# Experts sorted by token count: four passes of 128 slots with three products, four of 64 slots with two, in blocks of 1024 columns

## Chip, core and metric

The kernel runs on one core of one Trainium2 chip. The metric is the device time of one execution in microseconds (us), lower is better. Engines are named as in the profile: TensorE (PE, with its weight loads as PEld), VectorE (DVE), ScalarE (ACT), GpSimd (POOL), and SyncE (SP), which issues the weight loads from memory.

## What is computed

Two post-norm layers over 256 tokens of 1024 values, all in float32. Each has a mixer (pooling and mLSTM) and a channel mixer. The channel mixer of layer 0 is a dense SwiGLU, that of layer 1 takes two of eight experts for each token:

```python
N_EXPERTS = 8
TOP_K = 2
D_FF_EXPERT = 7 * D_MODEL // 2      # 3584

def swiglu(x, wg, wu, wd):
    return (jax.nn.silu(x @ wg) * (x @ wu)) @ wd

def moe_swiglu(x, w_router, b_router, wg, wu, wd):
    logits = (x @ w_router).astype(jnp.float32) + b_router.astype(jnp.float32)
    top_v, top_i = lax.top_k(logits, TOP_K)
    top_w = jax.nn.softmax(top_v, axis=-1)
    combine = jnp.sum(jax.nn.one_hot(top_i, N_EXPERTS, dtype=jnp.float32) * top_w[..., None], axis=-2)
    out = jnp.zeros_like(x)
    for e in range(N_EXPERTS):
        out = out + combine[..., e:e + 1] * swiglu(x, wg[e], wu[e], wd[e])
    return out
```

512 pairs of token and expert are spread over the eight experts as the router chooses. The biases of the router are drawn, so that experts get unequal numbers.

## The kernel before

Weights come from memory in units of 128 x 2048 values (1 MB). For each unit SP issues one transfer (`load`, L443), ScalarE rounds it into `w_hi` (`round_hi`, L644), VectorE subtracts that from the raw values into `w_lo` (`subtract_lo`, L865), and TensorE multiplies: a product in float32 is made of three matmuls in the rounded type, hi x hi, hi x lo, lo x hi (`product`, L1288 to L1292). Raw units lie in a ring of RING = 9 slots (7 of their own, RAW, and 2 in space that the expert stage does not use), and the pairs w_hi, w_lo in a ring of SPLIT = 3. ScalarE waits for the matmuls of the unit three before, VectorE for ScalarE, TensorE for VectorE, SP for VectorE's subtraction of the unit that had the slot (`slot_free`, L428). At the change from one item to the next, the first unit of the new item has the slot of unit 36 of the old one, of 42. Every engine has its own program in order.

An expert is one item, in the order 0 to 7. Its tokens are gathered into CAP = 104 slots; where an expert had more, further items are appended (MAX_OVER), for which GpSimd builds a table (`overflow_items`, L593, semaphore `table_ready` at L620). An item runs over seven blocks of 512 hidden columns. A block has two gate units, two up units (banks 2, 3 or 6, 7 in turn) and two down units, which stand one block later and add into banks 0 and 1. The tokens are the stationary operand (104 columns), the weights the moving one (512 columns), 12 matmuls a unit, 42 units an item. Between units stand, at steps written out by hand (STEP_ constants):

- silu of the gate bank by ScalarE (L824), product with the up bank by VectorE (L1232), four transposes by TensorE (L1617), the hi part of these by ScalarE (L829) and the lo part by VectorE (L1237);
- the scatter of the item before: sums `y_sb` (ScalarE, L841, two copies) times the slot matrix (L1576) and an addition into `work` for each quarter (L1218);
- picks for the next item by VectorE (`build_pick`, L1197: it waits for `table_ready`, then copies its table row at L1200 and compares at L1160 and L1162), and its gather (L1564): 16 float32 matmuls of tokens with the 0/1 pick matrix, recorded as 32, then hi and lo (L814, L1209).

Item 0 is written out; 1 to 7 are a loop. Before item 0 stand router, top two, positions (L1127 to L1172), the first picks and the first gather. In item 0, VectorE makes the tables (`item_tables`, L1175) after unit 4 and the scaled residual (`start_sums`, L1192, L1195) after unit 9. After item 7 come the last scatter, the last norm and the output.

## Time and profile before

| | |
|---|---|
| Time, median of 3 runs | 1494.95 us (1488.65 to 1495.79) |
| Span of the profiled execution | 1495.0 us |
| Busy: PE, PEld | 1434.3 us (96%), 1131.2 us (76%) |
| Busy: DVE, ACT, POOL | 1157.2 us (77%), 912.4 us (61%), 175.8 us (12%) |
| Granted TensorE clock, mean | 0.972 of full |
| Moved by DMA | 424.68 MB, mean 284 GB/s |

The span is cut by time: mixer 0, dense mixer and mixer 1 up to about 440 us, then the expert stage to 1476, then the tail. Busy PE says only that matmuls overlap in the records; what a matmul costs is the distance from one start to the next. An engine's idle time is given with what ended it.

### The profile page before, as it was taken

How to read it: one execution, taken by the hardware profiler on the slowest of the kernel's cores; microseconds unless marked ns; L12 is line 12 of the kernel's file. 1: busy time of each engine (PE TensorE's matmuls, PEld its weight loads, DVE VectorE, ACT ScalarE, POOL GpSimd, SP SyncE). 2: the span in 40 equal slices, each digit the busy share in tenths (PEclk: the TensorE clock that was granted, in tenths of full speed). 3: DMA queues.
4: the chain of work that ended last, by engine and by line, in shares of the span. 5: the costliest groups of instructions: out<-in, count | busy, mean ns of one | idle time of the engine just before them, and what ended most of it. 6: DMA issues, size and time to landing. Idle time of an engine off the chain costs nothing.

```text
span 1495.0 us, 19658 instructions
## 1 busy us (share of the span) xinstructions
PE 1434.3 (96%) x7356; PEld 1131.2 (76%) x7356; DVE 1157.2 (77%) x991; ACT 912.4 (61%) x736; POOL 175.8 (12%) x224
## 2 busy tenths in 40 slices
PE   8998999988989869999999999999999999999996
PEld 7888999977977647777777777777777777777773
DVE  6766545468578668887988888888798978878887
ACT  5434434446436646676767767677676776767664
POOL 4523000025524810000000000000000000000001
PEclk9998999989989979999999999999999999999998
DMA  9635555544348867997999899799799979979970
GB/s 333 233 117 172 194 176 194 185 153 144 111 156 311 321 226 247 394 394 259 381 394 346 293 393 394 243 394 395 277 360 396 387 250 395 393 254 385 393 289 30
DMA packets 182307, 424.68 MB, mean 284 GB/s; under 512 B 9280, under 2 KB 11616, under 8 KB 182256
## 3 DMA queue, kind: packets, MB, share of 16 engines
q1 hardware_dynamic: 180608, 419.17, 77.3%
q0 software_dynamic: 1504, 4.76, 1.0%
q8 instruction: 33, 0.54, 0.1%
q14 instruction: 18, 0.15, 0.0%
q10 hardware_dynamic: 144, 0.07, 0.0%
HBM read 422.92 MB, written 1.05 MB: 284 GB/s over the span
## 4 chain that ended last, share of the span: by engine, by line
PE 86%; DVE 6%; POOL 4%; issue 2%; ACT 1%; DMA 1%; SPq 0%; POOLq 0%; DVEq 0%; ACTq 0%
PE bank L1290 26%; PE bank L1292 26%; PE bank L1291 26%; PE bank L1564 2%; DVE w_lo L868 2%; POOL arena L599 2%; PE bank L1576 2%; PE bank L1617 1%; DVE arena L940 1%; DMA raw<-in_w_in 1%; PE bank L1427 1%; POOL arena L607 1%; PE bank L1311 0%; DVE x_lo L895 0%; DVE arena L938 0%
## 5 line engine op out<-in xcount | busy, mean ns | idle before, releaser
L868 DVE TENSOR_TENSOR w_lo<-raw,w_hi 128x2048 fp32r<-128x2048 f32 x335 | 767.8, 2295 | 234.9 <-ACT w_hi L649 231.5
L649 ACT CAST w_hi<-raw 128x2048 fp32r<-128x2048 f32 x335 | 639.7, 1910 | 249.4 <-PE bank L1292 246.1
L1290 PE MATMUL bank<-w_hi,parts 128*104 128x512 f32 (+1 forms) x1496 | 603.6, 403 | 17.2 <-DVE w_lo L868 17.1
L1292 PE MATMUL bank<-w_hi,parts 128*104 128x512 f32 (+1 forms) x1496 | 588.0, 393 | 0.0
L1291 PE MATMUL bank<-w_lo,parts 128*104 128x512 f32 (+1 forms) x1496 | 587.6, 393 | 0.0
L1290 PEld LDWEIGHTS bank<-w_hi,parts 128*104 128x104 f32 (+1 forms) x1496 | 254.5, 170 | 109.8 <-DVE w_lo L868 17.7
L1291 PEld LDWEIGHTS bank<-w_lo,parts 128*104 128x104 f32 (+1 forms) x1496 | 254.8, 170 | 92.6 <-issue 7.3
L1292 PEld LDWEIGHTS bank<-w_hi,parts 128*104 128x104 f32 (+1 forms) x1496 | 254.4, 170 | 90.6
L1290 PE MATMUL bank<-x_hi,w_hi 128*128 128x256 f32 x596 | 173.0, 290 | 1.4 <-ACT arena L707 1.4
L1291 PE MATMUL bank<-x_lo,w_hi 128*128 128x256 f32 x596 | 171.7, 288 | 0.0
L1292 PE MATMUL bank<-x_hi,w_lo 128*128 128x256 f32 x596 | 171.6, 288 | 0.0
L868 DVE TENSOR_TENSOR w_lo<-arena,w_hi 128x2048 fp32r<-128x2048 f32 x64 | 146.5, 2290 | 27.8 <-ACT w_hi L649 27.2
L586 POOL TENSOR_TENSOR tokens<-work,ln_row 128x1024 f32<-128x1024 f32 x7 | 16.6, 2370 | 1195.0 <-DVE work L1076 1195.0
L649 ACT CAST w_hi<-arena 128x2048 fp32r<-128x2048 f32 x64 | 122.3, 1911 | 43.9 <-PE bank L1292 43.9
L1290 PEld LDWEIGHTS bank<-x_hi,w_hi 128*128 128x128 f32 x596 | 117.9, 198 | 3.3 <-issue 3.0
L1291 PEld LDWEIGHTS bank<-x_lo,w_hi 128*128 128x128 f32 x596 | 117.7, 198 | 0.2
L1292 PEld LDWEIGHTS bank<-x_hi,w_lo 128*128 128x128 f32 x596 | 117.5, 197 | 0.0
L824 ACT ACTIVATE arena<-bank 104x512 f32<-104x512 f32 x56 | 33.5, 598 | 79.6 <-PE bank L1292 79.5
L829 ACT CAST parts<-bank 128x416 fp32r<-128x416 f32 x56 | 28.3, 506 | 54.1 <-PE bank L1617 54.1
L1564 PE MATMUL bank<-arena,tokens 128*128 128x104 f32 x288 | 37.2, 287 | 1.1 <-DVE arena L1160 1.1
L1232 DVE TENSOR_TENSOR arena<-arena,bank 104x512 f32<-104x512 f32 x56 | 38.1, 680 | 0.0
L1564 PEld LDWEIGHTS bank<-arena,tokens 128*128 128x128 f32 x288 | 36.5, 203 | 2.0 <-issue 1.1
(196 smaller groups left out, 809.0 us busy)
## 6 DMA issues: line engine op xcount, KB each, us to landing
raw<-in_wu_exp SPq DMA_DIRECT2D x96, 1024.0 KB, 7.4
raw<-in_wd_exp SPq DMA_DIRECT2D x96, 1024.0 KB, 7.1
raw<-in_wg_exp SPq DMA_DIRECT2D x80, 1024.0 KB, 7.0
arena<-in_wg_exp SPq DMA_DIRECT2D x32, 1024.0 KB, 7.6
raw<-in_w_in SPq DMA_DIRECT2D x20, 1024.0 KB, 6.7
arena<-in_wu_exp SPq DMA_DIRECT2D x16, 1024.0 KB, 9.4
arena<-in_wd_exp SPq DMA_DIRECT2D x16, 1024.0 KB, 9.1
raw<-in_wg_dense SPq DMA_DIRECT2D x11, 1024.0 KB, 5.1
```

What stands on the lines that cost most here:

```text
L586: st.then(g.tensor_tensor(tokens[:, t, :], work[:, t, :], ln_row[:, 0, :], ALU.mult))
L599: st.then(g.tensor_tensor(v[..., 0:n], v[..., 0:n], v[..., n:2 * n], ALU.add))
L649: a.copy(w_hi[:, n % SPLIT, :], slot(n)).then_inc(hi_ready, 1)
L824: a.activation(esg[0:CAP, b % 2, :], bank[(2, 6)[b % 2]][0:CAP, :], ACT.Silu) \
L829: a.copy(eh_hi[:, b % 2].rearrange("p j c -> p (j c)"), bank[5][:, 0:4 * CAP]) \
L868: v.tensor_tensor(w_lo[:, n % SPLIT, :], slot(n), w_hi[:, n % SPLIT, :].bitcast(F32), ALU.subtract).then_inc(lo_ready, 1)
L1232: v.tensor_tensor(eh[0:CAP, b % 2, :], esg[0:CAP, b % 2, :], bank[(3, 7)[b % 2]][0:CAP, :], ALU.mult).then_inc(eh_ready, 1)
L1290: mm(psum, left[0], right[0], start=first, stop=False)
L1291: mm(psum, left[0], right[1], start=False, stop=False)
L1292: return mm(psum, left[1], right[0], start=False, stop=last)
L1564: last = mm(psum[:, (k % 4) * CAP:(k % 4 + 1) * CAP], tokens[:, t, k * P:(k + 1) * P], pick[:, t, :], start=t == 0, stop=t == TT - 1)
L1576: mm(psum[:, :], scat[0:CAP, t * P:(t + 1) * P], y_sb[0:CAP, n * HALF:(n + 1) * HALF], start=True, stop=True).then_inc(scat_mm, 1)
```

## The change

- Experts are sorted by their token counts on the chip. The four largest take the even items (0, 2, 4, 6) with 128 slots and three matmuls a product as before; the four smallest take the odd ones with 64 slots. An expert that has more than its item holds gets a further item of 128 slots at the end (`n_over`).
- In a narrow item the hi part of 64 tokens and their lo part stand side by side as 128 stationary columns, so a product is two matmuls, with w_hi and w_lo (`one_pass`). The lower 64 rows of each gate and up bank are then copied by ScalarE to `fold` and added to the upper rows by a matmul with a shifted identity.
- The seven blocks of 512 columns become three of 1024 and one of 512. Gate is in banks 2 and 3, up in 6 and 7; copies, silu and products have up to 1024 columns. Of the sums there is one copy, of 1024 columns.
- Transposes of a wide block are made in two steps, into banks 5 and 4; their hi and lo parts are copied from there.
- Tokens are split once into `xt_hi` and `xt_lo` (ScalarE, VectorE), and the gather multiplies these, in the rounded type. Of the gathered tokens ScalarE copies both parts; VectorE has no step there, but for item 0.
- The table is made on VectorE in small steps after units 3 to 19 of item 0, and GpSimd has no part in it. SP waits for it before item 1 and takes each item's expert number from it.
- `start_sums` stands before item 0; after it the tokens' buffer serves as ninth raw slot. RAW is 6, RING stays 9.
- The loop holds two items, a narrow and a wide one.

The core of the diff (in `narrow_item`, the first is ScalarE's, the second VectorE's, the third TensorE's):

```diff
-EXP_BLOCKS = F_EXP // FBLK
+EBLK = 1024
+EXP_WIDTH = [EBLK, EBLK, EBLK, 512]
+EXP_BLOCKS = len(EXP_WIDTH)
...
-CAP = 104
-MAX_OVER = (TOP_K * T) // (CAP + 1)
...
+WIDE, NARROW = 128, 64
+ITEM_CAP = [WIDE, NARROW, WIDE, NARROW, WIDE, NARROW, WIDE, NARROW]
+ITEM_RANK = [0, 4, 1, 5, 2, 6, 3, 7]
+MAX_OVER = 4
...
+PAIRS = E // 2 - 1
...
-RAW = 7
-RING = RAW + 2
+RAW = 6
+RING = RAW + 3
...
+TURN = {10: 0, 20: 1, 32: 2, 38: 3}
+SCATTER = {2: 0, 4: 1, 6: 2, 8: 3}
+STEP_SLOTS, STEP_PICK = 16, 20
+GATHER = {33: 0, 38: 1}
+TAKE = {36: 0, 40: 1}
...
-        spare = [arena[:, ARENA - UNIT:], arena[:, 0:UNIT]]
+        spare = [arena[:, ARENA - UNIT:], arena[:, 0:UNIT], tokens[:].rearrange("p t d -> p (t d)")]
...
-                return w[:, 4 * b + 2 * half:4 * b + 2 * half + 2, :]
-            return w[:, 4 * half:4 * half + 4, b * FBLK:(b + 1) * FBLK]
+                k0 = EBLK // P * b + 2 * half
+                return w[:, k0:k0 + 2, :]
+            kn = UNIT // EXP_WIDTH[b]
+            return w[:, kn * half:kn * (half + 1), b * EBLK:b * EBLK + EXP_WIDTH[b]]
...
+                elif u == RAW + 2:
+                    sp.wait_ge(tokens_free, 1)
...
             item_loads(0, 0, first=True)
+            sp.wait_ge(table_ready, 1)
             with sp.Fori(1, E) as i:
-                item_loads(i, i)
-
-            sp.wait_ge(table_ready, 1)
-            n_over = sp.value_load(over_int[0:1, MAX_OVER:MAX_OVER + 1], min_val=0, max_val=MAX_OVER)
+                e = sp.value_load(order_int[0:1, bass.ds(i, 1)], min_val=0, max_val=E - 1)
+                item_loads(i, e)
...
-            overflow_items()
...
+            def token_high(t):
+                act.wait_ge(tokens_ready, TT * 2 + t + 1)
+                a.copy(xt_hi[:, t, :], tokens[:, t, :]).then_inc(xthi_ready, 1)
...
+            def take(i, n, wide):
+
+                hi, lo = GATHER_BANKS[n]
+                act.wait_ge(gather_mm, 2 * i + n + 3)
+                if wide:
+                    a.copy(four(xg_lo, n), bank[lo])
+                a.copy(four(xg_hi, n), bank[hi]).then_inc(xg_ready, 1)
+
+            def gate_silu(i, b, rows):
+
+                if b:
+                    act.wait_ge(eh_ready, i * EXP_BLOCKS + b)
+                w = EXP_WIDTH[b]
+                a.activation(esg[0:rows, 0:w], wide_bank(GATE, w, rows), ACT.Silu).then_inc(esilu, 1)
+
+            def slots(i):
+                act.wait_ge(st_mm, i + 1)
+                a.copy(scat[:], bank[4][:, 0:T]).then_inc(scat_ready, 1)
+
+            def item_sums(i):
+                act.wait_ge(unit_done, i * ITEM_UNITS + (MOE_UNIT0 + ITEM_UNITS))
+                a.copy(y_sb[:], wide_bank(0, D)).then_inc(ysb_ready, 1)
...
+            def narrow_item(i, p, wide_next):
+                for u in range(ITEM_UNITS):
+                    round_hi(MOE_UNIT0 + u + AHEAD, i)
+                    if u in GATE_END or u in UP_END:
+                        act.wait_ge(unit_done, i * ITEM_UNITS + (MOE_UNIT0 + u + 1))
+                        b, n = (GATE_END[u], GATE) if u in GATE_END else (UP_END[u], UP)
+                        w = EXP_WIDTH[b]
+                        c0 = HALF if n == UP and w == HALF else 0
+                        if n == UP and w > HALF:
+                            act.wait_ge(fold_mm, 2 * EXP_BLOCKS * p + 2 * b + 1)
+                        elif n == GATE and b:
+                            act.wait_ge(fold_mm, 2 * EXP_BLOCKS * p + 2 * b)
+                        a.copy(fold[NARROW:, c0:c0 + w], psum[NARROW:, n:n + 2, :].rearrange("p a b -> p (a b)")[:, 0:w]) \
+                            .then_inc(foldin_ready, 1)
+                    if u - 1 in GATE_END:
+                        b = GATE_END[u - 1]
+                        act.wait_ge(fold_mm, 2 * EXP_BLOCKS * p + (2 * b + 1))
+                        if b == 0:
+                            act.wait_ge(eh_ready, i * EXP_BLOCKS)
+                        gate_silu(i, b, NARROW)
+                    if u in TURN:
+                        b = TURN[u]
+                        n, j = EXP_WIDTH[b] // P, 8 if b == EXP_BLOCKS - 1 else 0
+                        act.wait_ge(eturn_mm, i * FILLS + turned_fills(b))
+                        a.copy(eh_hi[:, j:j + n, 0:NARROW],
+                               bank[5][:, 0:n * NARROW].rearrange("p (j c) -> p j c", c=NARROW)) \
+                            .then_inc(ehi_ready, 2 if b < EXP_BLOCKS - 1 else 1)
+                    if u == STEP_SLOTS:
+                        slots(i)
+                    if u in TAKE:
+                        act.wait_ge(unit_done, i * ITEM_UNITS + (MOE_UNIT0 + u))
+                        take(i + 1, TAKE[u], wide_next)
+                item_sums(i)
...
+            def token_low(t):
+                dve.wait_ge(xthi_ready, t + 1)
+                v.tensor_tensor(xt_lo[:, t, :], tokens[:, t, :], xt_hi[:, t, :].bitcast(F32),
+                                ALU.subtract).then_inc(xtlo_ready, 1)
+
+            token_low(0)
...
+                if u == 3:
+                    wide_slots(lambda t: posm[:, t, 0:1], lambda t: comb[:, t, 0:1])
+                    dve.wait_ge(count_mm, 1)
+                    v.tensor_copy(count, bank[0][:, 4 * E:5 * E]).then_inc(count_ready, 1)
+                elif u == 4:
+                    dve.wait_ge(count_ready, 1)
+                    st.then(v.tensor_tensor(key, count, cst[:, C_BIG:C_BIG + E], ALU.add))
...
+                elif u == 19:
+                    st.add(v.tensor_copy(order_int[:, 0:MAX_ITEMS], item_tab[:, 0:MAX_ITEMS, 4]))
+                    st.then(v.tensor_copy(order_int[:, MAX_ITEMS:], n_over_f))
+                    dve.sem_inc(table_ready, 1)
 
             def start_sums():
-
-                dve.wait_ge(tokens_ready, TT * 3)
...
+                dve.sem_inc(tokens_free, 1)
...
+            def hidden(i, b, rows):
+
+                dve.wait_ge(esilu, i * EXP_BLOCKS + (b + 1))
+                w = EXP_WIDTH[b]
+                v.tensor_tensor(eh[0:rows, 0:w], esg[0:rows, 0:w], wide_bank(UP, w, rows), ALU.mult) \
+                    .then_inc(eh_ready, 1)
...
+            def narrow_item(i, p, wide_next):
+                for u in range(ITEM_UNITS):
+                    subtract_lo(MOE_UNIT0 + u + AHEAD, i)
+                    if u - 1 in UP_END:
+                        b = UP_END[u - 1]
+                        dve.wait_ge(fold_mm, 2 * EXP_BLOCKS * p + (2 * b + 2))
+                        dve.wait_ge(eturn_mm, i * FILLS + 2 * b)
+                        hidden(i, b, NARROW)
+                    if u in TURN:
+                        b = TURN[u]
+                        n, j = EXP_WIDTH[b] // P, 8 if b == EXP_BLOCKS - 1 else 0
+                        dve.wait_ge(ehi_ready, i * FILLS + turned_fills(b))
+                        v.tensor_tensor(eh_hi[:, j:j + n, NARROW:],
+                                        bank[5][:, 0:n * NARROW].rearrange("p (j c) -> p j c", c=NARROW),
+                                        eh_hi[:, j:j + n, 0:NARROW].bitcast(F32),
+                                        ALU.subtract).then_inc(elo_ready, 2 if b < EXP_BLOCKS - 1 else 1)
+                    if u - 1 in SCATTER:
+                        add_scattered(i - 1, SCATTER[u - 1])
...
+            start_sums()
...
+            def gather_half(parts_, n, psum, width, c0):
+                for k in range(4 * n, 4 * n + 4):
+                    at_c = (k % 4) * P + c0
+                    for t in range(TT):
+                        last = mm(psum[:, at_c:at_c + width], parts_[:, t, k * P:(k + 1) * P], pick[:, t, 0:width],
+                                  start=t == 0, stop=t == TT - 1)
+                return last
+
+            def gather(i, n, wide):
+
+                hi, lo = GATHER_BANKS[n]
                 if n == 0:
                     pe.wait_ge(pick_ready, 2 * i + 2)
-                for k in range(4 * n, 4 * n + 4):
-                    for t in range(TT):
-                        last = mm(psum[:, (k % 4) * CAP:(k % 4 + 1) * CAP],
-                                  tokens[:, t, k * P:(k + 1) * P], pick[:, t, :], start=t == 0, stop=t == TT - 1)
-                last.then_inc(gather_mm, 1)
+                if wide:
+                    gather_half(xt_hi, n, bank[hi], P, 0)
+                    gather_half(xt_lo, n, bank[lo], P, 0).then_inc(gather_mm, 1)
+                else:
+                    gather_half(xt_hi, n, bank[hi], NARROW, 0)
+                    gather_half(xt_lo, n, bank[hi], NARROW, NARROW).then_inc(gather_mm, 1)
...
+            def one_pass(psum, left, right, first, last):
+                mm(psum, left, right[0], start=first, stop=False)
+                return mm(psum, left, right[1], start=False, stop=last)
...
+            def narrow_item(i, p, wide_next):
+                for u in range(ITEM_UNITS):
+                    unit(i, u, False, one_pass, lambda k: xg_hi[:, k, :], lambda j: eh_hi[:, j, :])
+                    if u - 1 in GATE_END or u - 1 in UP_END:
+                        b, up = (GATE_END[u - 1], 0) if u - 1 in GATE_END else (UP_END[u - 1], 1)
+                        w = EXP_WIDTH[b]
+                        c0 = HALF if up and w == HALF else 0
+                        pe.wait_ge(foldin_ready, 2 * EXP_BLOCKS * p + (2 * b + up + 1))
+                        for hf in range(w // HALF):
+                            last = mm(bank[(GATE, UP)[up] + hf], shift, fold[:, c0 + hf * HALF:c0 + (hf + 1) * HALF],
+                                      start=False, stop=True, skip_group_check=True)
+                        last.then_inc(fold_mm, 1)
...
+            for n in range(2):
+                gather_half(xt_hi, n, bank[FIRST_BANKS[n][0]], P, 0).then_inc(gather_mm, 1)
+            pe.wait_ge(xtlo_ready, TT)
+            for n in range(2):
+                gather_half(xt_lo, n, bank[FIRST_BANKS[n][1]], P, 0).then_inc(gather_mm, 1)
+            wide_item(0, False, first=True)
+            with pe.Fori(0, PAIRS) as p:
+                narrow_item(p * 2 + 1, p, True)
+                wide_item(p * 2 + 2, False)
+            narrow_item(E - 1, PAIRS, True)
```

## Rows read from the trace of the kernel before

**Rows 1.** The line of the sum copies: count, duration in ns, first and last start.

```profile
L841 ACT COPY arena<-bank x16: 571/584/590, 593.7 to 1476.5; 104x512 f32<-104x512 f32 x16
```

**Rows 2.** Busy time by stretch: item 0 and items 1 to 7.

```profile
core 0: us, PE busy (x) PEld busy (x) DVE busy (x) ACT busy (x) POOL busy (x), PEclk, DMA share, GB/s
452.00:594.00 142.00, 124.92 (x570) 92.02 (x569) 104.68 (x77) 87.44 (x60) 54.07 (x99) 0.94 0.76 272
594.00:1476.00 882.00, 882.00 (x4020) 645.25 (x4019) 755.05 (x477) 618.29 (x421) 0.00 (x0) 1.00 0.93 343
```

**Rows 3.** Waits from 600 to 1470: who waited for whom, total, times, longest.

```profile
ACT w_hi L649 <- PE bank L1292: 151.9, 180, 2.3
DVE w_lo L868 <- ACT w_hi L649: 122.2, 152, 2.7
```

**Rows 4.** Timeline of TensorE (start us, us): 104 columns of weights, then 128.

```profile
861.12 0.39 PE L1291 MATMUL bank<-w_lo,parts 128*104 128x512 f32 x1
...
861.81 0.39 PE L1291 MATMUL bank<-w_lo,parts 128*104 128x512 f32 x1
...
409.39 0.39 PE L1290 MATMUL bank<-w_hi,parts 128*128 128x512 f32 x1
...
410.07 0.39 PE L1290 MATMUL bank<-w_hi,parts 128*128 128x512 f32 x1
```

**Rows 5.** Chain and timeline: four transposes, 16 gather records, eight scatter records.

```profile
551.13 0.36 PE bank L1617 x4
...
568.46 1.79 PE bank L1564 x16
...
1478.69 3.69 PE L1576 MATMUL bank<-arena 104*128 104x512 f32 x8 [2.21 <-issue]
```

**Rows 6.** Timeline of VectorE and TensorE, and the chain, at the hole of item 0.

```profile
531.46 0.17 DVE L1200 COPY arena<-arena 128x4 f32<-128x4 f32 x1 [17.98 <-POOLq L620]
...
534.87 0.76 PE L1290 MATMUL bank<-w_hi,parts 128*104 128x512 f32 x1 [17.07 <-DVE w_lo L868]
...
536.05 0.43 PE bank L1292
```

**Rows 7.** DMA: a stretch of 50 us, and GB/s in 40 slices of 860 to 960.

```profile
1000.00:1050.00 50.00, 50.00 (x222) 35.89 (x221) 43.44 (x31) 34.24 (x24) 0.00 (x0) 1.00 1.04 394
...
GB/s 387 387 388 398 408 400 388 386 388 386 412 404 391 388 385 389 402 405 400 386 388 386 397 403 406 387 389 387 388 406 352 400 328 280 0 0 12 291 170 365
```

**Rows 8.** Timeline: two casts, and two subtractions, one behind the other.

```profile
436.70 3.71 ACT L649 CAST w_hi<-raw 128x2048 fp32r<-128x2048 f32 x2
...
483.76 4.48 DVE L868 TENSOR_TENSOR w_lo<-raw,w_hi 128x2048 fp32r<-128x2048 f32 x2
```

**Rows 9.** Groups by line and shape: busy us, mean ns, idle before them.

```profile
L868 DVE TENSOR_TENSOR w_lo<-raw,w_hi 128x2048 fp32r<-128x2048 f32 x335 | 767.8, 2295 | 234.9 <-ACT w_hi L649 231.5
L649 ACT CAST w_hi<-raw 128x2048 fp32r<-128x2048 f32 x335 | 639.7, 1910 | 249.4 <-PE bank L1292 246.1 <-DMA raw<-in_w_in 2.7
...
L1291 PEld LDWEIGHTS bank<-w_lo,parts 128*104 128x104 f32 x1344 | 226.3, 168 | 87.0 <-issue 7.3
...
L1291 PEld LDWEIGHTS bank<-w_lo,parts 128*128 128x128 f32 x152 | 28.6, 188 | 5.6
...
L1232 DVE TENSOR_TENSOR arena<-arena,bank 104x512 f32<-104x512 f32 x56 | 38.1, 680 | 0.0
```

**Rows 10.** Timeline at the start of item 0, and of `start_sums`.

```profile
445.99 0.17 DVE L1170 RECIPROCAL arena<-arena 128x2 f32<-128x2 f32 x1
446.19 0.36 DVE L1172 TENSOR_SCALAR arena<-arena 128x8 f32<-128x8 f32 x2
...
451.82 0.46 PE L1290 MATMUL bank<-w_hi,parts 128*104 128x512 f32 x1
...
481.98 1.25 DVE L1195 TENSOR_SCALAR work<-tokens 128x2048 f32<-128x2048 f32 x1
```

**Rows 11.** Busy time in a stretch of mixer 1 with holes.

```profile
335.00:345.00 10.00, 8.59 (x72) 8.41 (x71) 5.71 (x10) 9.74 (x12) 2.78 (x1) 1.00 0.01 2
```

534 lines of the change are left out of this document (302 added, 232 removed).

## The prediction, made before the changed kernel was seen

> **What bounds the kernel now.** I read the stretches first [rows 1, 2]. The 16 copies of item sums run from 593.7 to 1476.5 us, two for each of eight items, so seven items take 882 us, 126.0 each [rows 1]. In that stretch TensorE is busy in all 882 us at the full granted clock, VectorE in 755, ScalarE in 618, and DMA moves 343 GB/s [rows 2]. The waits say the same from the other side: ScalarE waits for matmuls 151.9 us, VectorE for ScalarE 122.2, and TensorE appears in no large row [rows 3]. So an expert item is bound by matmul issue. Matmuls of 512 columns start 0.23 us apart (0.69 for three) [rows 4]. One item has 42 units of 12 of them, 504: 115.9 us. Beside them lie 28 transposes at 0.09 (2.5), the gather's 32 records at 0.112 (3.6) and the scatter's 8 at 0.46 with the last one's tail, 0.43 without (3.4) [rows 5]: 125.4 of 126.0. The first item is different: from 452 to 594 TensorE has 17.1 us without work [rows 2], and that is one hole: VectorE stands 17.98 us at L1200 for the table that GpSimd builds, TensorE follows with 17.07, and then runs at the low clock, matmuls 0.43 apart [rows 6].
>
> The other three resources of an item, since they come next. DMA: 42 units of 1.049 MB are 44.0 MB; the rate that is held for 50 us is 394 GB/s, and in the slices it goes between 385 to 389 and 400 to 412 [rows 7]. The fast slices recur as often as the down units, which come in rows of 4 KB where gate and up units have 2 KB. Two thirds at 387 and one third at 404 make 112.2 us an item. VectorE: a subtraction behind another takes 2.19 (4.48 less 2.29), 42 of them 92.0. ScalarE: a cast behind another 1.80, 42 make 75.6 [rows 8, 9].
>
> **The hole in item 0 goes.** GpSimd's table work is removed; VectorE does some 35 small operations of at most 128 elements, or 320 in one reduction, spread over units 3 to 19. Small operations take 0.17, dependent ones start 0.20 apart [rows 6, 10]; about 18 dependent ones at 0.21 and the rest at about 0.1 are 5.5 us where the old tables had about 1. What hides them is VectorE's idle time in a wide item, 882 less 755 over seven, 18 us each [rows 2]; without it they would cost 4.5. I take 0.5. Gone: 17.1 of hole and the low clock behind it, about 12 matmuls at 0.43 in place of 0.23, 2.4. GpSimd is free there, so nothing is late next; SP's new wait for the table stands behind unit 41's load, which itself waits for unit 32, long after unit 19. **-19.0.**
>
> **Start of the items.** Behind the first picks VectorE now also subtracts half of the tokens (1024 columns, 1.2 by the line from 0.68 at 512 to 2.29 at 2048 [rows 9]) and scales all tokens (1.25, before hidden at 482 [rows 10]), and both first copies of gathered tokens must be there before unit 0, where before the second one was waited for at unit 1. Chain: the combine weights are done at 446.6 [rows 10]; +1.2, +1.25, subtraction 2.2, copy 0.6, subtraction 2.2, copy 0.6 = 454.7, against 451.8 where unit 0 started [rows 10]. **+3.0** (0 to +5; the second unit is then ready at once, which can give some back). The ninth load slot is now the tokens' buffer, free at about 449; it is needed at unit 8, some 25 us later: nothing. Mixer and dense units get 6 raw slots for 7. A dense unit has 24 matmuls of 512 columns or 48 of half the length, 24 x 0.227 = 5.4 us, against 2.7 for its load (1.049 MB at 394): nothing, to +2.
>
> **Wide items, four.** 504 products as before, now with 128 columns of weights in place of 104. The weight loads grow from 168 to 188 ns, but with 128 columns matmuls start 0.227 apart (0.68 for three) against 0.23 [rows 4, 9]: the load lies beside the matmul before it. 504 matmuls: -1.5 to 0. Transposes 28 at 0.11 for 0.09: +0.6. The gather in two rounded halves is 32 matmuls of one pass for 16 of two: the same 32 records, of 64 or 128 columns; no row has such a one, the bounds are 0.05 and 0.12, so -2.0 to +0.3, and I take -0.5, near the weight-load bound of the 0.112. One copy of 1024 columns (about 1.07) ends the item where one of 512 (0.58) did: +0.5 if it shows. Gate and up banks are single now, but their readers run four units before the next writer, 11 us against 1.2. ScalarE's silu of 1024 columns stands 1.07 between two casts: cast n starts when matmuls n-3 end, cast and subtraction take 4.2, plus 1.07 is 5.3 against the 5.5 that two units of matmuls last, so it fits by 0.2 us; a slip of half a microsecond at 8 places is the upper end. **+0.5 each** (-2 to +4): 126.5.
>
> By the Trainium skill, TensorE: Matmul & The Clock Gate, section LDWEIGHTS, a weight load takes time by its columns, P/1.2 ns, so 24 more columns cost 20 ns. The trace agrees on the load itself (188 less 168) and shows that it is hidden; were it exposed, 504 loads would be 10.1 us an item and the total some 1470; with 0.227 measured, that is within rival 6's chance.
>
> **Narrow items, four.** Hi and lo tokens stand side by side in the 128 columns, so a unit has 8 matmuls for 12. TensorE: 336 at 0.23 = 77.3; 14 matmuls that fold the lower rows up, 3.2; transposes, gather, scatter 9. Sum 89.5, so 36 us under what it had. It no longer binds; the next three are:
> - DMA: gate and up units of 1024 columns have rows of 4 KB, 38 of 42 units at 404 and 4 at 387: 109.5; at the old mix 112.2. The lead of a full ring (four to six landed units when a wide item ends) lends some 10 us.
> - VectorE: 92.0 + products 3 x 1.22 + 0.68 + lo parts 2.4 + scatter sums 4 x 0.68 + picks 1.2, less 0.08 for each that follows another: 102.
> - ScalarE: 75.6 + 8 fold copies (6 x 1.07 + 2 x 0.6; a copy of 512 columns takes 0.58 [rows 1], each column more is put at the cast's slope, 1910 for 2048 [rows 9]) + silu 3.8 + hidden, gathered and slot copies 5 + sums 1.07, less overlap: 91.
>
> None of these is reached, since the three work in a ring of three split slots: cast n waits for matmuls n-3. From the end of subtraction n-3: matmuls 1.84, cast 1.91, two semaphore steps about 0.1 each, 3.95 until subtraction n can start; VectorE wants it at 2 x 2.19 = 4.4. Slack 0.45. A gate block puts a fold copy (1.07) and a silu (1.07) between ScalarE's casts, VectorE has nothing of its own there: it loses 2.1 - 0.45 and gains a little back, 1.2. An up block puts one fold copy in, followed by VectorE's own product: 0.4. A turn of the hidden values makes ScalarE wait for matmuls of this unit and the transposes: 0.4. Four blocks: 8; the end of the item with take and sum copies 1.5 to 2. 102 + 10 = 112, beside DMA at 109.5 to 112.2: I take **113**, 13.0 less than 126.0. Bounds: 107 (half of the stalls, lead used up) and 122 (twice the stalls).
>
> **Tail.** The last sum copy is 1024 wide: +0.5.
>
> **Sum.** 1495.0 - 19.0 + 3.0 + 4 x 0.5 - 4 x 13.0 + 0.5 = 1429.5, forecast 1430. The profiled span of 1495.0 is the median of the runs shown (1494.95), so nothing is added.
>
> **Rivals.**
> 1. The coupling costs twice (narrow 120 to 124): silu waits for the fold, the fold for ScalarE's copy, that for the unit's matmuls, and the chain of waits goes round the ring. For: slack 0.45 against insertions of 1.07. Against: VectorE's own extras let ScalarE catch up. 4 x 8 more: 1462. Chance 0.22.
> 2. DMA binds. Only if what DMA showed here, a mean of 343 [rows 2], were near what it can give: 44.0 MB at 350 are 126, narrow gains nothing over that, 1480. Against it: 394 over 50 us [rows 7]. Chance 0.07.
> The Trainium skill, DMA: Bandwidth & Descriptors, section Where 436 GB/s comes from, has this rule: from HBM to SBUF the HBM side binds at about 358 GB/s a core. An item would last 123 and the total would be 1470. The trace disagrees, with 394.
> 3. The floors are reached, narrow 106 to 108: 1400 to 1410. Chance 0.08.
> 4. Slower: TensorE's clock. In a narrow item it has 89.5 us of work in 113, in holes of 0.3 to 0.9 us each unit. At the low level matmuls are 0.43 apart [rows 6], a unit 3.4, a narrow item about 165. It decides when narrow items average 131, that is, when 35% of their work is at the low clock: over 1502; all of it, 1640. Against: in 335 to 345 TensorE was busy in 8.59 of 10 us, with 72 matmuls, and kept 1.00 [rows 11], and a TensorE that falls behind has full work again. Chance 0.04.
> 5. It doesn't do what it says: the fifth most frequent expert has over 64 tokens, and a wide item is appended, +126.5: 1556. The reference's router on its own inputs (seed 0) gives 99, 90, 74, 59 and 53, 50, 49, 38, so no item is appended. Chance 0.02.
> 6. Small things eat the gain up to 1487 to 1502: 0.02.
>
> Forecast as worked out, 1412 to 1450: 0.55. The range reaches from rival 3 (1400) to the far side of rival 1 (1474) and leaves out somewhat under 2 in 10. Faster by over 0.5% (about what a measurement of this kernel can tell from no change, 7.5 us): 0.92; within: 0.03; slower: 0.05.
>
> **What would show it.** No wait of VectorE for GpSimd and no low clock near 520. First unit at about 455. Item sums alternating 126.5 and 113 apart; in the narrow stretches VectorE waits for ScalarE about 10 us, TensorE busy by count of matmuls only, DMA 385 to 395 GB/s. Landings late with a full queue would mean rival 2; a granted clock under 1.00 rival 4; a ninth item rival 5. The prediction is wrong if a narrow item lasts over 122 or a wide one over 130.

## The result, and the profile of the changed kernel

The changed kernel takes 1428.01 us (median of four runs, 1424.38 to 1430.79) against 1494.59 of the kernel before (1488.65 to 1495.79): ratio 0.9556, interval 0.9532 to 0.958. The forecast was 1430, in a range of 1400 to 1474. Its profiled execution has a span of 1428.8 us, 66.2 under the 1495.0 of before.

The page of after: the span, the busy time of each engine, and the DMA queue that the page lists third.

```profile
span 1428.8 us, 18212 instructions
...
PE 1317.5 (92%) x6740; PEld 1084.5 (76%) x6740; DVE 1142.5 (80%) x959; ACT 938.6 (66%) x743; POOL 124.2 (9%) x126
...
q8 instruction: 59, 0.97, 0.3%
```

TensorE lost 117 us of busy time, VectorE only 15, and ScalarE gained 26. The line of the sum copies, which cuts the expert stage into items (before: [rows 1]):

```profile
L860 ACT COPY arena<-bank x8: 1012/1020/1029, 577.9 to 1410.1; 128x1024 f32<-128x1024 f32 x8
```

Seven items lie between the first and the last of them, 832.2 us where there were 882. Read one by one in the timeline of ScalarE they are 113.0, 125.6, 114.0, 125.6, 115.5, 125.6 and 112.9 us long: wide 125.6, narrow 112.9 to 115.5. Busy time by stretch, after, where [rows 2] stood before: item 0, narrow item 1, wide item 2, narrow item 5.

```profile
core 0: us, PE busy (x) PEld busy (x) DVE busy (x) ACT busy (x) POOL busy (x), PEclk, DMA share, GB/s
452.00:578.00 126.00, 124.96 (x572) 102.40 (x573) 106.13 (x94) 87.47 (x57) 0.00 (x0) 0.99 0.89 325
578.00:691.00 113.00, 97.48 (x422) 70.60 (x421) 102.69 (x59) 93.74 (x65) 0.00 (x0) 1.00 0.97 379
691.00:817.00 126.00, 125.48 (x574) 101.85 (x572) 108.13 (x63) 89.15 (x58) 0.00 (x0) 1.00 0.95 363
1056.00:1172.00 116.00, 99.34 (x424) 72.40 (x424) 103.23 (x60) 94.19 (x65) 0.00 (x0) 0.99 0.97 371
```

In the wide item TensorE still works without a break (the 0.5 us that 691 to 817 lacks lie behind its last matmul). In the narrow one it has room, and so have ScalarE and DMA; VectorE is busy in 102.7 of 113.0 us. The waits of 578 to 691 (who waited for whom: us, times, longest) give the rest of VectorE's time:

```profile
PEld bank L1756 <- DVE w_lo L946: 21.7, 22, 2.1
PE bank L1756 <- DVE w_lo L946: 13.0, 17, 1.7
DVE w_lo L946 <- ACT w_hi L667: 10.2, 15, 1.3
ACT w_hi L667 <- PE bank L1757: 7.1, 7, 1.7
ACT parts L896 <- PE bank L1757: 7.0, 6, 2.4
```

102.7 + 10.2 = 112.9. All three engines wait for one another here: TensorE for VectorE, VectorE for ScalarE, ScalarE for TensorE. So no engine alone sets the time; whether the way round this ring does is what the experiments ask. One gate block in the timeline of ScalarE (start us, us, in brackets the idle time before):

```profile
642.67 1.01 ACT L896 CAST parts<-bank 64x1024 fp32r<-64x1024 f32 x1 [1.72 <-PE bank L1757]
643.71 1.92 ACT L667 CAST w_hi<-tokens 128x2048 fp32r<-128x2048 f32 x1
645.65 1.02 ACT L852 ACTIVATE arena<-bank 64x1024 f32<-64x1024 f32 x1
646.57 5.50 ACT L667 CAST w_hi<-raw 128x2048 fp32r<-128x2048 f32 x3
```

And VectorE beside it:

```profile
645.65 2.29 DVE L946 TENSOR_TENSOR w_lo<-tokens,w_hi 128x2048 fp32r<-128x2048 f32 x1 [0.88 <-ACT w_hi L667]
648.49 6.69 DVE L946 TENSOR_TENSOR w_lo<-raw,w_hi 128x2048 fp32r<-128x2048 f32 x3 [0.54 <-ACT w_hi L667]
655.97 2.29 DVE L946 TENSOR_TENSOR w_lo<-raw,w_hi 128x2048 fp32r<-128x2048 f32 x1 [0.79 <-ACT w_hi L667]
```

ScalarE waits for the unit's matmuls, copies the lower rows (1.01), casts, does silu (1.02), casts again. VectorE loses 0.88 behind the copy and 0.54 behind silu, 1.42 for the gate block where 1.2 was forecast. The 0.79 of the last row lies behind the copy of the up block (ScalarE, 652.99).

By stages (us; the two profiled executions):

| | forecast | measured |
|---|---|---|
| Mixers and dense layer | 0 | -2.3 (executions of one kernel differ as much) |
| Start of the items | +3.0 | +3.1 |
| Item 0, first matmul to last sum copy | -18.5 | -17.5 (142.8 to 125.3) |
| Narrow items, four | -52.0 | -48.6 (504.0 to 455.4) |
| Wide items 2, 4, 6 | +1.5 | -1.2 |
| Tail | +0.5 | +0.2 |
| Sum | -65.5 | -66.3 |

So the total is right within the noise, and two terms are off by some 3 us in opposite directions.

### The profile page after: what moved, and what is told of

The parts are those of the page before. It is cut to its first block, busy times and chain, and to the rows that moved or that the text cites. A ratio compares the mean times of both kernels' runs of the same rounds, so it can differ in the third digit from the quotient of the medians.

```text
span 1428.8 us, 18212 instructions
## 1 busy us (share of the span) xinstructions
PE 1317.5 (92%) x6740; PEld 1084.5 (76%) x6740; DVE 1142.5 (80%) x959; ACT 938.6 (66%) x743; POOL 124.2 (9%) x126
## 4 chain that ended last, share of the span: by engine, by line
PE 67%; DVE 15%; ACT 8%; issue 8%; DMA 1%; SPq 0%; ACTq 0%; DVEq 0%
PE bank L1456 17%; PE bank L1458 17%; PE bank L1457 17%; DVE w_lo L946 9%; ACT w_hi L667 6%; PE bank L1756 4%; PE bank L1757 4%; PE bank L1728 2%; PE bank L1752 2%; DVE arena L1018 1%; PE bank L1821 1%; DVE arena L1361 1%; DMA raw<-in_w_in 1%; ACT arena L852 1%; PE bank L1593 1%
## 5 line engine op out<-in xcount | busy, mean ns | idle before, releaser
L946 DVE TENSOR_TENSOR w_lo<-raw,w_hi 128x2048 fp32r<-128x2048 f32 x303 | 692.6, 2299 | 202.0 <-ACT w_hi L667 200.6
L667 ACT CAST w_hi<-raw 128x2048 fp32r<-128x2048 f32 x303 | 575.0, 1910 | 232.4 <-PE bank L1458 205.9
L1456 PE MATMUL bank<-w_hi,parts 128*128 128x512 f32 x824 | 332.0, 403 | 4.6 <-DVE w_lo L946 2.4
L1756 PE MATMUL bank<-w_hi,parts 128*128 128x512 f32 x672 | 281.6, 419 | 55.7 <-DVE w_lo L946 54.3
L1458 PE MATMUL bank<-w_hi,parts 128*128 128x512 f32 x824 | 322.1, 391 | 0.0
L1457 PE MATMUL bank<-w_lo,parts 128*128 128x512 f32 x824 | 321.8, 391 | 0.0
L1757 PE MATMUL bank<-w_lo,parts 128*128 128x512 f32 x672 | 264.5, 394 | 0.0
L1756 PEld LDWEIGHTS bank<-w_hi,parts 128*128 128x128 f32 x672 | 126.6, 188 | 121.2 <-DVE w_lo L946 86.9
L1456 PEld LDWEIGHTS bank<-w_hi,parts 128*128 128x128 f32 x824 | 155.2, 188 | 44.2 <-DVE w_lo L946 8.0
L1457 PEld LDWEIGHTS bank<-w_lo,parts 128*128 128x128 f32 x824 | 155.3, 188 | 33.1 <-issue 2.9
L1458 PEld LDWEIGHTS bank<-w_hi,parts 128*128 128x128 f32 x824 | 155.0, 188 | 33.3
L1757 PEld LDWEIGHTS bank<-w_lo,parts 128*128 128x128 f32 x672 | 126.9, 189 | 27.0 <-issue 3.6
L946 DVE TENSOR_TENSOR w_lo<-tokens,w_hi 128x2048 fp32r<-128x2048 f32 x32 | 73.3, 2290 | 16.0 <-ACT w_hi L667 15.9
```

The costliest lines, as they stand in the source:

```text
L667: a.copy(w_hi[:, n % SPLIT, :], slot(n)).then_inc(hi_ready, 1)
L946: v.tensor_tensor(w_lo[:, n % SPLIT, :], slot(n), w_hi[:, n % SPLIT, :].bitcast(F32), ALU.subtract).then_inc(lo_ready, 1)
L1456: mm(psum, left[0], right[0], start=first, stop=False)
L1457: mm(psum, left[0], right[1], start=False, stop=False)
L1458: return mm(psum, left[1], right[0], start=False, stop=last)
L1756: mm(psum, left, right[0], start=first, stop=False)
```

## The experiments

All times are medians, of two runs for e3, e4, e7, e8 and e12 and of one for e10; the kernel before had 1493.5 to 1493.8 beside them. An item is measured from sum copy to sum copy. Edits are on the changed kernel unless the text says otherwise.

### The hole of item 0 alone

`e1_short_table` is the kernel before with a short table for GpSimd.

```diff
-MAX_OVER = (TOP_K * T) // (CAP + 1)
+MAX_OVER = 1
```

> The kernel before with MAX_OVER = 1 in place of 4: GpSimd builds one row of the table of further items in place of four, so the table is there about 46 us earlier (it was built from 469.6 to 531.2, some 15 us a row). Nothing else changes. If the hole of item 0 and the low clock behind it are worth 19.5 us, as in the sum of the prediction: 1494.6 - 19.5 = 1475, no wait of VectorE for GpSimd. Rival: the hole hides something else (DMA or the ring catches up in it), and less than 10 us are gained: over 1485.

Measured: 1471.85 us, ratio 0.9862 (0.984 to 0.9884). From the first subtraction of item 0 to that of item 1 it takes 126.8 us for 146.4, so 19.6 less. VectorE's wait for GpSimd is gone, and GpSimd's work is hidden:

```profile
446.00:571.00 125.00, 125.00 (x585) 92.96 (x585) 107.32 (x77) 88.62 (x62) 28.45 (x27) 1.00 0.88 317
```

The hole and the low clock behind it are worth the 19.5 of the forecast before its deduction. The medians differ by 21.9, 2 us more, which no view places: the part ahead of item 0 differs by several us between executions.

### Wide items, and the jump back

`e2_all_wide` makes every item wide, two in a loop as in the changed kernel.

```diff
-ITEM_CAP = [WIDE, NARROW, WIDE, NARROW, WIDE, NARROW, WIDE, NARROW]
+ITEM_CAP = [WIDE] * 8
...
-                narrow_item(p * 2 + 1, p, True)
-                wide_item(p * 2 + 2, False)
-            narrow_item(E - 1, PAIRS, True)
+                wide_item(p * 2 + 1, True)
+                wide_item(p * 2 + 2, True)
+            wide_item(E - 1, True)
```

> The changed kernel with all eight items wide (128 slots, three products); sorting, table, blocks of 1024 columns and split gather stay. If the narrow items alone bring what is beyond the hole and the small terms: 1428 + 4 x (125.6 - 113.9) = 1475, as much as the kernel before without its hole, and every item 125.6 apart. If the blocks of 1024 columns or the 4 KB rows bring something of their own in a TensorE-bound item, it is under 1470; if the order of the items matters (a narrow item ahead lends a wide one something), over 1480.

Measured: 1482.58 us, ratio 0.9926 (0.9909 to 0.9942), 8 more than expected and past the 1480 at which the order of the items would matter. Items take 125.5, except two: items 3 and 5, at 129.8 and 129.9. They are the first of the second and the third turn of the loop. TensorE's timeline of e2 at item 3, where the loop jumps back:

```profile
826.11 0.39 PE L1458 MATMUL bank<-w_hi,parts 128*128 128x512 f32 x1
829.04 0.79 PE L1456 MATMUL bank<-w_hi,parts 128*128 128x512 f32 x1 [2.54 <-DVE w_lo L946]
829.63 0.63 PE L1457 MATMUL bank<-w_lo,parts 128*128 128x512 f32 x1
830.05 0.63 PE L1458 MATMUL bank<-w_hi,parts 128*128 128x512 f32 x1
```

The subtraction named as releaser had ended at 825.34, 3.7 us before; what came last was something else. Then matmuls are 0.43 apart for 3 us: the clock had fallen to its low level in the stop. At 826.4 the trace has a packet of the queue "instruction". The changed kernel stops as long at items 3 and 5:

```profile
819.03 0.49 PE L1756 MATMUL bank<-w_hi,parts 128*128 128x512 f32 x1 [2.55 <-DVE w_lo L946]
...
1055.69 0.39 PE L1458 MATMUL bank<-w_hi,parts 128*128 128x512 f32 x1
1058.61 0.49 PE L1756 MATMUL bank<-w_hi,parts 128*128 128x512 f32 x1 [2.53 <-DVE w_lo L946]
```

At item 3 matmuls go on 0.23 apart and the item is 1.1 us longer than in e9 below; at item 5 they are 0.43 apart from 1059.66 on, and it is 2.6 longer. The stop is the same, the clock behind it is not.

My theory was now that the engine fetches its program from memory there, since a loop of two items doesn't stay in its instruction store. In 720 to 1400 us, the DMA view of e2:

```profile
q1 hardware_dynamic: 66476, 236.52, 92.7%
q8 instruction: 29, 0.48, 0.3%
```

`e11_wide_loop_of_one` is e2 with one item in the loop, on all three engines.

```diff
-            with pe.Fori(0, PAIRS) as p:
-                wide_item(p * 2 + 1, True)
-                wide_item(p * 2 + 2, True)
-            wide_item(E - 1, True)
+            with pe.Fori(1, E) as i:
+                wide_item(i, True)
```

> All eight items wide as in e2_all_wide, but the loop holds one item, not two, as in the kernel before. There items 3 and 5, behind the jump, lasted 129.8 us, the others 125.5. If the size of the loop's body is the cause (two items do not stay in the instruction memory, one does): all items 125.5, total 1482.6 - 8.6 = 1474, no instruction packets of queue q8 after the second turn. If the jump as such costs it: 6 jumps of 4.3 us, over 1490.

Measured: 1477.22 us, ratio 0.989 (0.9875 to 0.9905). All items take 125.5 to 125.6, and first to last sum copy takes 879.0 us where e2 had 887.1. The same stretch of the DMA view of e11:

```profile
q1 hardware_dynamic: 67362, 239.97, 93.6%
```

There the queue for instructions doesn't appear, as it doesn't in the same stretch of the kernel before. So the jump back of a loop with two wide items costs some 4 us (129.8 and 129.9 for 125.5). The median is 5.4 under that of e2, where the items account for 8, and 3 over the expected 1474; the first sum copy came 4 us later in e11's profiled execution.

`e9_unrolled` has the changed kernel's items without a loop, on all three engines; SyncE keeps its own.

```diff
-            with pe.Fori(0, PAIRS) as p:
+            for p in range(PAIRS):
```

> The changed kernel with the loops over pairs of items written out on ScalarE, VectorE and TensorE (SP keeps its loop); the work is the same. In the changed kernel the two items behind the jump back to the loop's head last 114.0 and 115.5, the other narrow ones 113.0 and 112.9. If the jump costs this, by the fetch of TensorE's instructions at a target that is no longer held: every narrow item 113, total 1428 - 3.6 = 1424. If the excess is of loads or of chance: 1427 to 1429, with one or two narrow items at 114 to 116 again. If straight code were fetched late everywhere: over 1430.

Measured: 1424.1 us, ratio 0.9549 (0.9532 to 0.9565, five runs). All four narrow items take 112.8 to 112.9, and first to last sum copy 827.8 for 832.2. The median is 3.9 under that of the changed kernel, and the two intervals overlap; the item lengths are what shows the gain. TensorE's timeline of e9 at the start of item 5 has no gap:

```profile
1051.20 0.39 PE L1458 MATMUL bank<-w_hi,parts 128*128 128x512 f32 x1
1051.42 0.39 PE L1756 MATMUL bank<-w_hi,parts 128*128 128x512 f32 x1
```

It fetches too (23 packets in 720 to 1400), with no loss: what costs is the fetch after a jump, not that in a straight line. That the fetch is TensorE's own is read from the packet at the time of its stop; no run gave the longer loop to TensorE alone.

### What a narrow item's 113 us are

Four theories: the ring with its insertions (mine), DMA's transfers, VectorE alone, and TensorE with its clock. The first run leaves the insertions out: no fold copies and no matmuls that add them.

```diff
-                        a.copy(fold[NARROW:, c0:c0 + w], psum[NARROW:, n:n + 2, :]...) \
-                            .then_inc(foldin_ready, 1)
```

> The changed kernel; in narrow items the fold is left out (ScalarE's eight copies of the lower rows and the 14 matmuls that add them), so the products with the lo tokens are missing. Ring theory: of about 10 us of stalls in a narrow item those of the fold go, some 6, ScalarE has 8 us less, and the item falls from 113.9 to about 108 or to DMA's own time, 109.5; total 1405 to 1412. DMA theory (loads bind the narrow item at 113): 113 stays, total 1424 to 1428.

Measured: 1404.86 us, ratio 0.9408 (0.9374 to 0.9441). Narrow items take 106.2, 107.1, 108.6 and 106.3, wide ones 125.5. Busy time of the stretch of item 1 in e3:

```profile
581.00:688.00 107.00, 95.24 (x411) 68.67 (x410) 102.68 (x60) 86.99 (x57) 0.00 (x0) 1.00 1.03 401
```

VectorE's wait for ScalarE in the same stretch:

```profile
DVE w_lo L939 <- ACT w_hi L667: 4.6, 8, 1.3
```

6.8 us less an item in the mean, and in item 1 VectorE's wait is 5.6 less (10.2 to 4.6). DMA moved 401 GB/s with its engines busy all the time (share 1.03), which is 42.9 MB in 107 us; the rest of the item's 44.0 had landed before. So the 109.5 us that I had set for DMA are no floor for an item that starts with landed units, though its rate of 404 was about right.

The second run halves what each unit loads, from item 1 on (half of the rows of `dst`; the other half of a slot keeps older weights).

```diff
+                if n >= MOE_UNIT0 and not first:
+                    dst, src = dst[:, 0:k // 2, :], src[:, 0:k // 2, :]
```

> The changed kernel; from item 1 on each load brings only half of its rows of weights (the other half of the slot keeps what it had), so DMA has half its bytes. Ring theory: narrow items stay at 113 to 114, wide at 125.6, total 1425 to 1428. DMA theory: narrow items fall to VectorE's 103 to 108, total under 1412.

Measured: 1425.12 us, ratio 0.9543 (0.9516 to 0.9571). Narrow items take 113.0, 113.3, 113.4 and 112.9. Busy time of item 1 in e4:

```profile
574.00:687.00 113.00, 97.56 (x422) 70.57 (x421) 102.63 (x60) 93.71 (x65) 0.00 (x0) 1.00 0.62 188
```

VectorE's wait for ScalarE in the same stretch:

```profile
DVE w_lo L948 <- ACT w_hi L669: 10.8, 16, 1.3
```

Half of the traffic, the same 113 us and about the same wait (10.8 for 10.2): DMA falls as a cause. The extra time at the jump back is down to 0.3 and 0.4 us here. The stop itself is not gone. TensorE's timeline of e4 at item 5:

```profile
1052.90 0.49 PE L1758 MATMUL bank<-w_hi,parts 128*128 128x512 f32 x1 [1.95 <-DVE w_lo L948]
```

It lasts 1.9 at both jumps where the changed kernel has 2.5, and matmuls go on 0.23 apart behind it. So half of the weights' traffic less takes some 0.6 us off the stop, and most of it stays. The rest of what item 5 gains is that the low clock stays away here, in one profiled execution.

The third run doubles each fold copy, 7.5 us more work for ScalarE in an item, and nothing for TensorE or VectorE.

```diff
+                        a.copy(esg_twice[:, 0:w], psum[NARROW:, n:n + 2, :]...)
                         a.copy(fold[NARROW:, c0:c0 + w], psum[NARROW:, n:n + 2, :]...) \
```

> The changed kernel; in narrow items ScalarE copies the lower rows twice (once more into unused rows), 8 copies or 7.5 us more per item. Ring theory: nearly all of it shows, since the slack is used up: 6 to 8 us a narrow item, total 1452 to 1460. DMA theory or slack in ScalarE (93.7 busy of 113): under 2 us an item, total up to 1436.

Measured: 1449.26 us, ratio 0.9705 (0.9677 to 0.9733). Narrow items take 118.5, 121.1, 119.7 and 118.4; against the changed kernel's that is 5.6 more in the mean, three quarters of what was added and a little under the 6 to 8 expected. Busy time of item 1 in e8:

```profile
575.00:693.00 118.00, 97.72 (x420) 69.92 (x418) 102.50 (x59) 99.44 (x72) 0.00 (x0) 1.00 0.96 363
```

VectorE's wait for ScalarE in the same stretch:

```profile
DVE w_lo L948 <- ACT w_hi L668: 15.8, 16, 1.9
```

ScalarE has 18.6 us idle in it and yet the item is longer, by just what VectorE's wait grew (10.2 to 15.8).

Then TensorE's share of the way round. `e7_one_matmul` leaves out the product with w_lo in narrow items, 4 matmuls a unit for 8.

```diff
-                mm(psum, left, right[0], start=first, stop=False)
-                return mm(psum, left, right[1], start=False, stop=last)
+                return mm(psum, left, right[0], start=first, stop=last)
```

> The changed kernel; in narrow items the matmul with w_lo is left out, one matmul a product, 336 less an item by half. Ring theory: cast n waits for the matmuls of unit n-3, so 0.9 us less per unit gives the ring slack; the stalls shrink from 10 us, the item falls to 107 to 111 with DMA's 109.5 the next bound; total 1400 to 1417. Rival that ScalarE and VectorE only queue among themselves and TensorE is out of the loop: no change, 1428. The clock may fall with so little work: then rows at 1.2 GHz show.

Measured: 1435.78 us, ratio 0.9615 (0.9538 to 0.9691). Less work and no gain, where 1400 to 1417 was expected; narrow items take 115.4, 112.7, 116.0 and 111.2. Busy time of items 1 and 2 in e7:

```profile
579.00:694.00 115.00, 83.48 (x251) 56.43 (x251) 102.01 (x60) 92.75 (x65) 0.00 (x0) 0.73 0.96 371
694.00:820.00 126.00, 125.31 (x573) 101.69 (x571) 108.17 (x63) 89.15 (x58) 0.00 (x0) 1.00 0.95 361
```

The clock went up and down in the narrow item (mean 0.73) and stayed up in the wide one, so matmuls at 0.43 took the place of those left out. The run says nothing about the ring; it shows that what rival 4 feared can happen, with the 4 matmuls a unit of this run and not with the 8 of the changed kernel.

`e12_two_more_matmuls` goes the other way: in narrow items each unit repeats the first matmul of its last product twice, into its own bank (bank 1 for a down unit).

```diff
+                if times is one_pass:
...
+                    for _ in range(2):
+                        last = mm(*again, start=False, stop=True, skip_group_check=True)
```

> The changed kernel; in each unit of a narrow item the last matmul with w_hi is issued two times more, so its product counts three times; 84 matmuls or 19 us more of TensorE in an item where it has 23 us without work. Ring theory: cast n waits for the matmuls of unit n-3, so 2.3 + 1.9 + 0.2 = 4.4 from one subtraction to the next but two leaves no slack at 4.4; every insertion shows in full, and the item lasts 4 to 12 us longer: total 1444 to 1476. Rival, that ScalarE and VectorE alone set the time of a narrow item: under 1 us an item, total 1428 to 1432.

Measured: 1455.38 us, ratio 0.9746 (0.9728 to 0.9764). Narrow items take 118.9, 120.4, 120.4 and 118.7. Busy time of item 1 in e12:

```profile
581.00:700.00 119.00, 113.62 (x506) 87.20 (x505) 103.34 (x59) 94.58 (x64) 0.00 (x0) 1.00 0.95 364
```

VectorE's wait for ScalarE in the same stretch:

```profile
DVE w_lo L946 <- ACT w_hi L667: 15.8, 19, 1.9
```

A unit's matmuls last 0.45 longer, which is the slack that the forecast gave the ring; 42 times that is 19 us, and 5.9 came out in item 1, within the 4 to 12 expected. So TensorE is part of the way round, at a third of its price. It is busy in 113.6 of 119 us here, so not far from binding by itself; what says that the item is longer through the ring is VectorE's wait (10.2 to 15.8). With e8 this settles it: ScalarE's insertions and TensorE's matmuls both reach the end of an item through VectorE's wait.

### Which expert is where

`e5_five_narrow` makes item 6 narrow too, to see whether several narrow items in a row are longer because the lead of the full ring is used up.

```diff
-ITEM_CAP = [WIDE, NARROW, WIDE, NARROW, WIDE, NARROW, WIDE, NARROW]
+ITEM_CAP = [WIDE, NARROW, WIDE, NARROW, WIDE, NARROW, NARROW, NARROW]
...
-PAIRS = E // 2 - 1
+PAIRS = 2
...
-            narrow_item(E - 1, PAIRS, True)
+            narrow_item(5, 2, False)
+            narrow_item(6, 3, False)
+            narrow_item(7, 4, True)
```

> The changed kernel with five narrow items and three wide: items 0, 2, 4 are wide, 1, 3, 5, 6, 7 narrow (the fourth largest expert has 59 tokens, so 64 slots hold it). Ring theory (VectorE's 102 us plus stalls by ScalarE's insertions): each narrow item lasts 113 to 114 whatever was before it, total 1428 - 11.7 = 1416. DMA theory (a narrow item is as fast as the loads let it, with a lead from the wide item before it): items 6 and 7 have no lead to draw on and last longer than items 1, 3 and 5, 116 or more, and the total is 1421 or more.

Measured: 1540.26 us, ratio 1.0306 (1.0289 to 1.0323). A ninth item appeared, 125.6 us long, and it turned the expected gain of 12 us into a loss of 112 against the changed kernel. Items 5, 6 and 7, narrow in a row:

```profile
1061.00:1173.00 112.00, 96.68 (x419) 70.10 (x417) 102.11 (x59) 92.55 (x63) 0.00 (x0) 1.00 0.97 379
1173.00:1285.00 112.00, 97.56 (x420) 70.64 (x420) 103.02 (x60) 92.68 (x63) 0.00 (x0) 1.00 1.01 394
1285.00:1398.00 113.00, 97.67 (x421) 70.76 (x422) 103.89 (x60) 94.06 (x65) 0.00 (x0) 1.00 1.00 391
```

112.3, 112.3 and 112.9: the lead is not needed. But by my table of counts (99, 90, 74, 59 and so on) item 6 would have held 59 tokens, and no item should have been added. The key by which the table sorts is `cst[:, C_BIG:C_BIG + E]` plus the count, and C_BIG is 1000 for expert 0 only. So expert 0 (50 tokens) always stands first, the next three wide places take 99, 90 and 74, and the narrow ones 59, 53, 49 and 38. In e5 item 6 had the 74, too many for 64. The description ahead of the prediction, "the four largest take the even items", is wrong. `e10_count_probe` counts on the chip: it tells the table that every item holds 64, so each expert above that gets a further item.

```diff
-    c[:, C_CAP:C_CAP + E] = ITEM_CAP
+    c[:, C_CAP:C_CAP + E] = NARROW
```

> The changed kernel, but an item counts as overfull when its expert has over 64 tokens, the wide ones too; each such expert gets a further wide item (with wrong slots, so its part of the output is wrong). Each adds 125.5 us. With the counts that the prediction names for seed 0 (99, 90, 74, then 59) it is three: 1428 + 377 = 1805. e5_five_narrow ran an item more than those counts allow; if the fourth count is over 64 in the data on the chip it is four: 1930.

Measured: 1809.79 us (one run), with three items of 125.6 us appended. Three experts have over 64 tokens, as the counts say.

### A version that beats both

Since expert 0 always has item 0 and fits into 64 slots here, item 0 can be narrow. `e13_first_narrow` is e9 with this (the first item's tables and first gather are adapted; on other inputs an expert 0 with over 64 tokens would get a further item).

```diff
-ITEM_CAP = [WIDE, NARROW, WIDE, NARROW, WIDE, NARROW, WIDE, NARROW]
-ITEM_RANK = [0, 4, 1, 5, 2, 6, 3, 7]
+ITEM_CAP = [NARROW, WIDE, NARROW, WIDE, NARROW, WIDE, NARROW, NARROW]
+ITEM_RANK = [0, 1, 4, 2, 5, 3, 6, 7]
```

> e9_unrolled with the first item narrow as well: five narrow items (0, 2, 4, 6, 7) and three wide (1, 3, 5). Item 0 always holds expert 0, because its weights are fetched before the counts are known; in this data it has 50 tokens and had a wide item to itself. (It serves inputs in which expert 0 has at most 192 tokens.) Ring theory: a wide item of 125.6 becomes a narrow one of 113, plus some 2 to 4 us since VectorE's table steps (some 5 us) now lie in an item that VectorE bounds, less its four missing additions: 1424 - 12.6 + 3 - 1.5 = 1413, in 1409 to 1418. If an item of over 64 tokens were left over, one more wide item: 1538. If the ring theory missed what the wide item of 0 hid (tables, first gather, new weights): over 1418.

Measured: 1413.89 us, ratio 0.9459 (0.944 to 0.9477, five runs), 14 us under the changed kernel. Item 0, from first subtraction to that of item 1, takes 121.4 for 131.2 in the changed kernel; e9 already had 3.9 of the 14. Its stretch:

```profile
448.00:567.00 119.00, 100.64 (x428) 74.39 (x428) 105.17 (x91) 93.50 (x65) 0.00 (x0) 0.95 0.93 345
```

That is 6 us over the 113 of the other narrow items. VectorE is busy in 105.2 us here for 102.7, since in a narrow item the small operations of the table have less to hide behind; its waits for ScalarE are 13.2 for 10.2, one of them 5.8 long; and its first matmuls are 0.43 apart, at the low clock (mean of the stretch 0.95).

## Why the prediction was right, and where not

- **Bound.** Right. A wide item is matmul issue: 125.6 us with no idle time of TensorE.
- **Hole of item 0.** Right: -19.6 in e1. In the changed kernel item 0 lost 17.5, 1.0 less than forecast. A term was missing: the first matmul stood behind 1.92 us of idle time and ran at the low clock. The timeline of TensorE, after (before, the unit began at full clock, [rows 10]):

```profile
452.61 0.76 PE L1456 MATMUL bank<-w_hi,parts 128*128 128x512 f32 x1 [1.92 <-issue]
453.17 0.63 PE L1457 MATMUL bank<-w_lo,parts 128*128 128x512 f32 x1
453.60 0.63 PE L1458 MATMUL bank<-w_hi,parts 128*128 128x512 f32 x1
```

  From there to the end of two units, at 459.46, it takes 6.85 us, where 24 matmuls at 0.227 are 5.45.
- **Start.** Right: from the same step of VectorE's top two (L1222, before L1138) to the first matmul of item 0 it took 12.9 us for 9.8, +3.1. The first unit stood at 452.6 and not near 455, because the part ahead ended 2.3 us earlier.
- **Wide items.** The weight loads of 128 columns are hidden, as forecast, and matmuls are 0.227 apart, the good end of "-1.5 to 0". The half a microsecond for slips of silu didn't come: 125.6 measured, 126.5 forecast, 0.9 too much for each of three (item 0 is counted above). The 1470 that the prediction gives for weight loads in the open was put under rival 6, whose 1487 to 1502 don't contain it.
- **Narrow items.** Value right, 113 forecast, 112.9 where nothing disturbs, and for the reason given: VectorE 102 and 10 us of stalls were forecast, 102.7 and 10.2 measured, and e3, e8 and e12 move the stalls. How the 10 is made up was forecast less well. In the timelines of VectorE and ScalarE over item 1 the four gate blocks cost 4.6 (4.8 forecast) and the ends of the item 2.0 (1.5 to 2). But the four up blocks cost 2.9 where 1.6 was forecast, and the four turns of the hidden values 0.3 where 1.6 was. That these two errors cancel is luck. The bounds 107 and 122 hold; e3 reaches the lower one only without the fold. Rival 1's 120 us and more are reached only with work added to the ring (e8, e12).
- **The missed term.** Items 3 and 5 took 114.0 and 115.5: the loop's jump back, 3.7 us over both, against e9. The prediction's parts have no term for the change from a loop of one item to one of two. The 3.4 of the narrow items and the 1.0 of item 0 are nearly cancelled by the 2.7 of the wide items and the 2.3 of the first part, so the total of 1428 is closer than its terms, by luck.
- **DMA.** "404 for rows of 4 KB" was about right as a rate: 401 GB/s were held over e3's item. As a floor of an item 109.5 us was wrong, since with its lead e3's took 106.2 to 108.6; the prediction has this lead and puts it in its lower bound. e4 shows that DMA doesn't bind at 113, and the changed kernel moved 371 to 379 GB/s in items 1, 3 and 5 where 385 to 395 was the sign named. Rival 2 falls. The DMA view of after in 40 slices of 720 to 1400 us; its best slices have 409 to 411, the kernel before has 394 to 397 in the same stretch:

```profile
GB/s 409 409 370 365 176 384 408 409 409 391 394 236 387 409 410 408 365 365 180 378 409 401 381 376 403 247 383 410 409 408 379 350 207 350 411 410 409 405 399 150
```

- **The clock.** Rival 4 did not come about, but e7 shows that halving the 8 matmuls of a unit would have brought it.
- **Rival 5.** No item was added, for the right counts but with a wrong picture of which expert is where, as e5 made plain. Whoever builds on "the four largest" goes wrong, as I did in e5: 1541.1 in the profiled execution for the 1428.8 of the changed kernel.

## What to carry to other kernels

When a loop binds through a ring of engines, work out the slack of the way round, and count an insertion on any of its engines at what it exceeds that slack; taking work away from one engine can move the bound to the ring and not to the next engine (112.9 us here, where VectorE was busy in 102.7). The total of the stalls came out here; their places did not, so go through a timeline before building on one of them. Before a loop's body is made longer, look at whether the queue for instructions appears in the DMA view, and compare the first item after each jump back with the others. Work out who gets which place in a sorted table from the key in the code, with the data's numbers, and not from what the sorting is called.

## What the runs showed of the hardware

- **Fetching the program.** A body with some 573 matmuls and as many weight loads (e11, kernel before) repeats with no packet in the instruction queue. One with two items fetches all the time (29 packets of 16 KB in 680 us of e2) and stops TensorE for 2.5 us at the jump back, 4.3 us an item with the low clock behind it. With half of the weights' traffic the stop is 1.9 us (e4). The wait is put down to a subtraction that had long ended.
- The Trainium skill, Advanced Engine Details and Errata, section ISA Cache, gives TensorE 128 KB, and 16 KB for 256 instructions; by that its store would hold some 2048 instructions, an estimate. The runs agree, but only bracket it. An item of the kernel before, which repeats without a fetch, has 574 + 574 matmuls and weight loads in its trace and 69 records of TensorE's sequencer (register, semaphore and branch), 1217 in all. Items 3 and 4 of the changed kernel, one turn of its loop, have 1988 and 126, 2114 in all; two wide ones have about 2290 without the sequencer's.
- **DMA.** Rows of 4 KB bring 409 to 411 GB/s in the best slices of 17 us, those of before 394 to 397, and 401 were held over a whole item of 107 us.
- **The clock.** Item 1, 113 us long, kept a granted clock of 1.00 with 8 matmuls of 512 columns a unit; with 4 (e7, 115 us) the mean was 0.73. Of two equal stops, 2.55 us ahead of item 3 and 2.53 ahead of item 5, only the second was followed by matmuls 0.43 apart.
